# The recurrence's drive with u as the stationary operand, turned back by transposes

## The reference

```
bu_re = einsum("blgh,gph->blgp", u, bb_re)
bu_im = einsum("blgh,gph->blgp", u, bb_im)
h     = associative_scan(h' = a * h + bu)          # over the 256 positions
y     = Re(C h) + D * u
```

## Time and profile before

| | us |
|---|---|
| median of three runs | 1013.58 |
| the profiled execution | 1013.73 |
| its span, first to last instruction | 1011.9 |
| TensorE busy | 996.7 (98%) |
| VectorE busy | 786.0 (78%) |
| ScalarE busy | 508.6 (50%) |
| GpSimd busy | 370.3 (37%) |

### The profile page before, as it was taken

The page is one execution under the profiler, slowest core; times in us unless marked ns, Lnnn a source line. Parts: engine busy times, 40 slices in busy tenths (PEclk is TensorE's granted clock), DMA queues, the critical chain, the costliest instruction groups (busy, mean ns, idle before and its releaser), DMA issues.

```text
span 1011.9 us, 15359 instructions
## 1 busy us (share of the span) xinstructions
PE 996.7 (98%) x5269; PEld 846.4 (84%) x5269; DVE 786.0 (78%) x1192; ACT 508.6 (50%) x702; POOL 370.3 (37%) x579
## 2 busy tenths in 40 slices
PE   8999999999999999999999999999999999999996
PEld 6888888899988888888878888888998788888885
DVE  5555666699877888996779978877998688787865
ACT  5544343475745444444555444445646454444453
POOL 6888999710127888980008600001002000000001
PEclk9999999999999999999999999999999999999999
DMA  9856555432456756565635565563334564646541
GB/s 280 256 175 206 167 200 175 163 126 84 174 163 201 229 192 207 166 223 192 204 129 184 186 212 199 174 223 114 121 126 167 191 209 148 241 157 216 190 163 42
DMA packets 143419, 181.56 MB, mean 179 GB/s; under 512 B 18384, under 2 KB 125584, under 8 KB 143376
## 3 DMA queue, kind: packets, MB, share of 16 engines
q1 hardware_dynamic: 143088, 180.48, 53.6%
q10 hardware_dynamic: 288, 0.52, 0.1%
HBM read 179.93 MB, written 1.05 MB: 179 GB/s over the span
## 4 chain that ended last, share of the span: by engine, by line
PE 97%; DVE 1%; ACT 1%; DMA 0%; issue 0%; POOL 0%; SPq 0%; POOLq 0%; ACTq 0%; DVEq 0%
PE ps L1462 30%; PE ps L1464 30%; PE ps L1463 30%; PE ps L1477 1%; PE ps L1757 1%; PE ps L1583 1%; PE ps L1740 1%; PE ps L1741 1%; PE ps L1710 1%; DMA raw<-in_ffn_w_up_dram 0%; DVE wL L789 0%; PE ps L1606 0%; ACT wH L430 0%; DVE xres L830 0%; PE ps L1626 0%
## 5 line engine op out<-in xcount | busy, mean ns | idle before, releaser
L789 DVE TENSOR_TENSOR wL<-raw,wH 128x1024 fp32r<-128x1024 f32 x336 | 425.9, 1311 | 56.1 <-ACT wH L430 54.9
L430 ACT ACTIVATE wH<-raw 128x1024 fp32r<-128x1024 f32 x336 | 336.1, 1051 | 101.9 <-PE ps L1464 95.6
L1462 PE MATMUL ps<-wH,uH 128*128 128x512 f32 x832 | 327.2, 393 | 3.7 <-DVE wL L789 2.5
L1464 PE MATMUL ps<-wH,uL 128*128 128x512 f32 x832 | 324.1, 390 | 0.0
L1463 PE MATMUL ps<-wL,uH 128*128 128x512 f32 x832 | 323.9, 389 | 0.0
L1462 PEld LDWEIGHTS ps<-wH,uH 128*128 128x128 f32 x832 | 156.2, 188 | 37.5 <-DVE uL L816 3.2
L1464 PEld LDWEIGHTS ps<-wH,uL 128*128 128x128 f32 x832 | 156.2, 188 | 32.9
L1463 PEld LDWEIGHTS ps<-wL,uH 128*128 128x128 f32 x832 | 156.3, 188 | 31.3
L1462 PE MATMUL ps<-wH,hTH 128*128 128x512 f32 x352 | 138.0, 392 | 0.0
L1464 PE MATMUL ps<-wH,hTL 128*128 128x512 f32 x352 | 137.2, 390 | 0.0
L1463 PE MATMUL ps<-wL,hTH 128*128 128x512 f32 x352 | 137.0, 389 | 0.0
(11 more groups left out here) (190 smaller groups left out, 1098.1 us busy)
## 6 DMA issues: line engine op xcount, KB each, us to landing
raw<-in_ffn_w_down_dram SPq DMA_DIRECT2D x88, 512.0 KB, 4.0
raw<-in_ffn_w_gate_dram SPq DMA_DIRECT2D x86, 512.0 KB, 4.0
raw<-in_ffn_w_up_dram SPq DMA_DIRECT2D x86, 512.0 KB, 5.0
raw<-in_w_in_dram SPq DMA_DIRECT2D x32, 512.0 KB, 4.4
raw<-in_w_out_dram SPq DMA_DIRECT2D x16, 512.0 KB, 3.8
raw<-in_ple_w_gate_dram SPq DMA_DIRECT2D x16, 512.0 KB, 4.0
raw<-in_glu_w_dram SPq DMA_DIRECT2D x4, 512.0 KB, 3.8
raw<-in_ple_w_proj_dram SPq DMA_DIRECT2D x4, 512.0 KB, 3.8
```

Of the source, the lines that this page charges most:

```text
L430: nc.scalar.activation(wH[:, slot, w], raw[:, slot, w], ACT.Copy).then_inc(wh_done, 1)
L789: nc.vector.tensor_tensor(wL[:, slot, w], raw[:, slot, w], wH[:, slot, w].bitcast(F32), ALU.subtract).then_inc((wl_half, wl_done)[a], 1)
L1462: mul(o, sH, vH, start=start, stop=False)
L1464: return mul(o, sL, vH, start=False, stop=stop)
```

## The change

`drive(h)` makes `u4[:, b, :]` (64 columns) the stationary operand and moves the 128 columns of `ETr` or `ETi`. Even blocks land in partitions 0 to 63, odd ones in 64 to 127. The result has the chunks along the partitions and the state along the columns. ScalarE copies the two banks of a half to `dlT`, and TensorE turns them back with eight transposes a half, `turn_drive(h)`, into the same banks, where `rotate_in` reads them as before. `turn_drive(0)` stands between units 1 and 2, `turn_drive(1)` in the middle of unit 3. On VectorE `rotate_out(0)` is moved ahead of the split of unit 4.

```
+        dlT = bufA[:, 0:1024]
 ...
+                def drive_evac(h):
+                    act.wait_ge(du_ps, l * 2 + (h + 1))
+                    if h == 1:
+                        act.wait_ge(dl_ps, l * 2 + 1)
+                    for n in range(2):
+                        nc.scalar.activation(dlT[:, 512 * n:512 * n + 512], ps[:, 2 + 2 * n + h, :], ACT.Copy).then_inc(dle_done, 1)
 ...
                 split_at(l, U_IN + 3)
+                drive_evac(0)
                 act.wait_ge(kc_full, l + 1)
                 place_taps(0)
                 drive_in(1)
                 split_at(l, U_IN + 4)
                 place_taps(1)
+                drive_evac(1)
                 place_taps(2)
 ...
                 scan(l, 0)
+                rotate_out(l, 0)
                 split_at(l, U_IN + 4)
-                rotate_out(l, 0)
                 rotate_in(l, 1)
 ...
-                    for b in range(8 * h, 8 * h + 8):
-                        c = slice(NCK * (b % 8), NCK * (b % 8) + NCK)
-                        mul(ps[:, 2 + h, c], ETr[:, b, :], u4[:, b, :], start=True, stop=True)
-                        last = mul(ps[:, 4 + h, c], ETi[:, b, :], u4[:, b, :], start=True, stop=True)
+                    for p in range(4):
+                        for n in range(2):
+                            for e in range(2):
+                                b = 8 * h + 2 * p + e
+                                last = mul(ps[64 * e:64 * e + 64, 2 + 2 * n + h, P * p:P * p + P], u4[:, b, :],
+                                           (ETr, ETi)[n][:, b, :], start=True, stop=True)
+                    last.then_inc(du_ps, 1)
+
+                def turn_drive(h):
+                    for n in range(2):
+                        pe.wait_ge(dle_done, l * 4 + (2 * h + n + 1))
+                        for p in range(4):
+                            at = 512 * n + P * p
+                            last = nc.tensor.transpose(ps[:, 2 + 2 * n + h, P * p:P * p + P], dlT[:, at:at + P], ident[:])
                     last.then_inc(dl_ps, 1)
 ...
                 w_in_unit(l, 1, lambda: drive(0))
+                turn_drive(0)
                 w_in_unit(l, 2)
                 drive(1)
-                w_in_unit(l, 3)
+                w_in_unit(l, 3, lambda: turn_drive(1))
                 outputs(0)
```

More of the change, by code:

```diff
@@ L222, in trunk @@
             sem("rsx_done"), sem("ems_done"), sem("z_out"), sem("u4a_done"), sem("u4d_done"))
+        du_ps, dle_done = sem("du_ps"), sem("dle_done")
         diag_done, rsb_ps, rsb_done, us_done = sem("diag_done"), sem("rsb_ps"), sem("rsb_done"), sem("us_done")
```

## The result

The changed kernel takes 1018.01 us (median of six runs, 1017.72 to 1018.32), the kernel before 1013.65 in the same sets of runs. The ratio is 1.0043, with a 95% interval of 1.0032 to 1.0054: it is slower by 4.4 us, where 3.8 were forecast. TensorE's own work did shrink, and VectorE's row of work starts later and passes this on.

A forecast was written before the change was run, and what follows sets the result against it. TensorE, 98% busy, and VectorE were taken as both full in the mixer. Stalls of 3.44 us a layer against 1.44 gained and 0.08 idle gave 1.92; two layers +3.8 on 1013.6, so 1017.4 us, full range 1014.8 to 1019.4.

The forecast's parts named there:

- The price of the parts: On TensorE, a half's new drive costs 2.01 us and its eight transposes 0.87, against 3.64 and 3.56 for the old drives.
- Both dear rivals: On TensorE: 64-column calls cost what the old did (1020.6 us, 6%), or transposes take their single length, 0.27 (1020.2, 3%).
- The slip: VectorE's `rotate_in(0)` must wait for the drive to be turned back, so VectorE's row starts 2.16 us later.
- The stalls: TensorE waits before the second drive (1.36 us), unit 4 (1.16), the GLU (0.22) and the GLU's fourth block (0.70).
- the walk: Six numbered steps following TensorE's meetings with late results, from `drive(1)` to the GLU's fourth block; lag 1.92 us a layer.
- The last wait: At the GLU's fourth block TensorE waits 0.70 us for `b_evac(1)`, bringing its lag to 1.92 a layer.
- Covered edits: ScalarE's copies for `turn_drive(1)` end at 234.3, just before TensorE arrives at 234.4: 0.1 us to spare.
- The cap: The wait for `b_evac(1)` limits any TensorE gain: 0.7 us a layer even with VectorE starting 0.43 earlier, 1012.2 us.
- The rival at 261.67: VectorE's idle 1.70 us there takes back most of its lateness, leaving a lag of 1.00 a layer: 1015.6 us, 12%.
- The clock: Sign of being wrong: a granted clock below full in TensorE's stalls, which would make all dearer; no size given.

The follow-up runs named there:

- the turning earlier: Changed kernel with `turn_drive(0)` moved 1.44 us forward, after 12 of the 24 matmuls of unit 1's second half: 1015.01 us.
- u first: Changed kernel with `scaled_u(1)` and `drive_in(1)` ahead of `rotate_in(0)` on VectorE: 1015.90 us.
- the kernel with the slip of 2.85: Kernel before, old drive, no transposes; VectorE's `rotate_in(0)` waits in addition for the end of unit 1 of W_in: 1020.93 us.
- the kernel with the shorter stalls (0.6 us): Kernel before, old drive; `rotate_in(0)` waits in addition for the 18th of 24 matmuls of unit 1's second half: 1018.08 us.

## Why the prediction was right, step by step

- *The price of the parts.* A drive of 2.01 us and transposes of 0.79 to their follower were read from L1757 and L1765; measured 2.00 and 0.79. Both dear rivals fall with this. The Trainium skill, "TensorE: Matmul & The Clock Gate", section on the PE-mode transpose, gives some 275 ns for one transpose. As a price for each of a run this trace does not bear it out: eight in a row took 0.79.
- *The slip.* Forecast 2.16, measured 2.21, and 2.26 at `b_evac(1)`: `rotate_out(0)` now follows its scan directly and exposes some of its wait (its move was costed at nothing).
- *The stalls.* 1.36, 1.16, 0.22 and 0.70 in the walk (the numbered steps of the prediction), as gaps between issues. The trace counts idle time from the end of the last matmul and has 1.27, 1.14 and 0.40, with a start at the GLU that was 0.24 late and left no row. As gaps between issues the measured ones are 1.43, 1.20, 0.24 and 0.55. Their sum, 3.42, is nearly the 3.44 of the walk, and that is partly luck: the first is larger than forecast, the last smaller. The places are as forecast, and so is the engine, since VectorE's copies ended after ScalarE's at the first.
- *The last wait decides.* The lag was taken as the last wait's, 1.92 a layer; measured 2.1 to 2.2. The experiments with the old drive (same slip, same time) and with the turning earlier show it, and u first agrees. Mis-sized was the term for what stands around a wait: the slip's 0.05, `rotate_out`'s 0.05, and a restart, after which the next two matmuls start 0.22 apart instead of 0.12. Over two layers this is most of the 0.6 us between the forecast of +3.8 and the measured +4.4.
- *Covered edits.* `drive_evac(1)` ran from 233.35 and was done at 234.44, `turn_drive(1)` started at 234.57, with no idle time before it: covered by 0.13, forecast 0.1.
- *The cap.* It was argued that no gain over 0.7 us a layer could pass VectorE's row. The kernel without the turning gained 0.64.
- *The rival at 261.67* had 12%; the idle 1.70 us stayed, to within a hundredth (1.71 and 1.70).
- *The clock* was named only as something that would make it dearer. In the changed kernel it stayed full in all six runs (mean 0.997 or 0.998); in the stall experiments it did not always.

What stays open is why the clock fell after one stall of 1.3 us and not after others of the same length, and whether GpSimd's additions alone stretch `rest_y`; neither was tried by itself.

## What to carry to other kernels

In this kernel a cheaper form on the engine that is 98% busy gained nothing, since it makes the result later for an engine that is nearly as full behind it. Walk the second engine's row to the last point where the first one waits for it, and take that lag, not the sum of the stalls; it also caps what any saving can bring. If the form is worth having, first make room at those waits, by order where that is enough, and find each next one: here five waits had to go (before the second drive, before unit 4, for `gelu_L(0)`, for `b_evac(1)` and for `rest_y`) before 2.9 us of saved matmul time showed up as 2.7.

## What the runs showed of the hardware

A call of plain fp32 operands took 0.22 us with a stationary of 128 columns and 64 columns moved (16 calls in 3.56), and 0.12 with a stationary of 64 columns and 128 moved (16 calls in 1.90, 229.69 to 231.59). Eight 128x128 transposes in a row took 0.79, one every 0.1, though each lasts some 0.27.

In the kernel with the slip of 2.85 the granted clock of TensorE fell to the lower level for some 7 us. This was 1.4 us after the end of an idle stretch of 1.3 us, in a kernel that is otherwise 98% busy, and it cost about 2 us; in the other layer of the same run a stall of the same length did nothing. In the kernel with the shorter stalls (0.6 us) one run of four had a lower mean clock and was 1.2 us longer. VectorE's `rest_y` instructions of 128x256 took 1.2 us each instead of 0.4 while GpSimd added in the same stretch.
